# Interleaving the identity matmuls with the half-width matmuls of the SSD output, and moving two regions of on-chip memory

## The chip, the cores and the metric

The kernel runs on one core of a Trainium2 chip. The metric is the device time of one execution in microseconds (us), the median of three runs. Engines are named as in the profile: PE is TensorE's matmul side and PEld its loading of stationary operands, DVE is VectorE, ACT is ScalarE, POOL is GpSimd, SP issues the DMAs. A matmul here multiplies a stationary operand, which is loaded first, by a moving operand, which is streamed, and adds the product into a bank of PSUM, the accumulation memory. A 4-byte float matmul that is not marked as the reduced form appears as two passes in the trace.

## The reference

The program is one sequence of 256 tokens, width 1024, through two models' blocks: two layers with a three-branch attention mixer and two layers whose mixer joins multi-head latent attention with an SSD (state space) branch; every layer has a gated feed-forward before and behind the mixer. The change is in the SSD branch, whose scan works in two chunks of 128 tokens, four groups of eight heads:

```python
def step(state, inp):
    xc, dtc, bc, cc = inp
    acum = jnp.cumsum(dtc * a_g, axis=1)
    decay = jnp.exp(jnp.where(causal, acum[:, :, None] - acum[:, None, :], -jnp.inf))
    cb = jnp.einsum('btgn,bsgn->btsg', cc, bc)
    xdt = xc * dtc[..., None]
    y_diag = jnp.einsum('btsg,btsgh,bsghp->btghp', cb, decay, xdt)
    y_off = jnp.einsum('btgn,bghpn->btghp', cc, state) * jnp.exp(acum)[..., None]
    ...
    return new_state, y_diag + y_off
```

For the first chunk the state is zero and y_off vanishes; for the second chunk y is the sum of both terms.

## The kernel before

Twelve phases run one after the other: feed-forward (`ffn`), mixer (`m1` or `m2`), feed-forward, for each of four layers. The two `m2` phases hold the SSD branch. All weights, 459 MB, are streamed once through a ring of five buffers, RAW. Each weight is split into a high part WHI (ACT, line 1438) and a rest WLO (DVE, line 2342), and each product is three matmuls, high times high (L378), high times low (L379) and low times high (L380), with XH and XL the split activations; in `m2` phases a stretch of these weight matmuls stands between any two small steps. Each engine's instructions are written out by hand in their order; an engine waits on counters ("signals") that others raise. Nothing reorders them.

The SSD branch takes its four groups g one after the other. `sttr` (L1041) transposes the convolved input XSB through the identity matrix, which lies in CF; DVE makes XDT from it (L3072); `le` (L1066) spreads the cumulated decays, ACT exponentiates them, and DVE multiplies them with CBM into LE (L3088). `yp` (from L1068) then forms y for one group and one chunk c: for each of the four pairs of heads, b = 0 to 3, two matmuls (h = 0, 1) with a stationary operand of 64 columns of XDT, one writing PSUM partitions 0 to 63 and the other 64 to 127, each 128 columns wide (L1086). Pairs 0 and 1 lie in bank 2, pairs 2 and 3 in bank 3. The second chunk also needs y_off. DVE has left it in JUNK (L3081), tokens along the partitions, and four matmuls with JUNK as a full stationary operand of 128 columns and the identity as the moving one (L1080) turn it and put it into the same columns of the banks. So `yp` of the second chunk, in this text "the block", is 4 matmuls of the one kind and 8 of the other. There are 8 blocks: 4 groups in each of 2 phases.

Behind a block DVE reads the sum from the bank (`yw`, L3097, into WT), waiting for the block's last matmul; for group 3 ACT also waits for it (L2057). In the next group `yp` waits for LE (L3088) and `sttr` waits for XSB (L2931) or for XDT of the chunk before (L3072).

On-chip tensors are placed by hand by their byte address in a partition. Up from 16,512 follow RAW (WLO shares it), WHI, X, XH and XL; then JUNK; then the constants CF, CM and some small ones up to SM2; then, at M0, one overlay region of some 97 KB which each phase lays out for itself (SG, HF, HH, HL of the feed-forward; LE, XDT, XSB, YH, YL, OHA, OHB and others of the mixers).

Of the kernel before, what the change touches and what calls it, by code (L numbers as in the profile page):

```python
# [5 lines left out]
F32 = mybir.dt.float32  # L6
# [8 lines left out]
P = 128  # L15
# [75 lines left out]
class Signals:  # L91
# [10 lines left out]
    def up(self, name, *key, by=1):  # L102
        if name not in self.sem:
            self.sem[name], self.owner[name] = self.ctx.enter_context(self.nc.semaphore(name)), self.engine
            self.count[name] = 0
        assert self.owner[name] == self.engine, name
        self.count[name] += by
        if not self.known:
            assert not key or (name,) + key not in self.value, (name, key)
            self.value[(name,) + key] = self.count[name]  # L110
        return self.sem[name], by

    def at(self, name, *key):
        return (self.sem[name], self.value[(name,) + key]) if self.known else (None, 1)
# [21 lines left out]
class Counts:  # L136
# [6 lines left out]
    def before(self, member, distance):  # L143
# [33 lines left out]
M2_SQUARE = Counts([("lat", j, t) for j in range(3) for t in range(2)] + [("q", j, t) for j in range(3) for t in range(2)]  # L177
                   + [("k", t, h) for t in range(2) for h in range(2)] + [(kind, g) for g in range(4) for kind in ("wx", "yo")])
# [4 lines left out]
def build(nc, phases, x_in, pos_in, w_in, cf_in, cm1_in, cm2_in, out, ctx):  # L183
    START = 16512
    top = [START]

    def sb(name, shape, dt, at=None):
        n = 2 if dt == BF16 else 4
        for s in shape[1:]:
            n *= s  # L190
        n = (n + 31) // 32 * 32
        if at is None:
            at = top[0]
            top[0] += n
        ends.append((at + n, name))
        return nc.alloc_sbuf_tensor_at(name, shape, dt, offset=at)
# [5 lines left out]
    X = sb("X", [P, 2, D], F32)  # L202
    XH = sb("XH", [P, 8, 256], F32R)
    XL = sb("XL", [P, 8, 256], F32R)
    JUNK = sb("JUNK", [P, 2, 512], F32)
    CF = sb("CF", [P, CF_W], F32)
    CM = sb("CM", [P, CM1_W], F32)
    IDB = sb("IDB", [P, P], BF16)
# [7 lines left out]
    SM = sb("SM", [P, 512], F32)  # L216
    SM2 = sb("SM2", [P, 456], F32)
    KRD, WST, EAC, CWH, SNH = [SM2[:, a:z] for a, z in ((0, 256), (256, 288), (288, 320), (320, 440), (440, 456))]
    IDN, TRI, ONE = CF[:, C_IDN:C_IDN + P], CF[:, C_TRI:C_TRI + P], CF[:, C_ONE:C_ONE + P]
    M0 = top[0] + (START - top[0]) % 1024  # L220
    K = 1024

    def at_kb(kb):
        return M0 + int(kb * K)

# [37 lines left out]
    XDT = sb("XDT", [P, 2, 512], F32, at_kb(50))  # L263
# [5 lines left out]
    LE = sb("LE", [P, 2, 1024], F32, at_kb(58))  # L269
# [16 lines left out]
    PS = [ctx.enter_context(nc.psum_tensor(f"bank{i}", [P, 512], F32)) for i in range(8)]  # L286
# [67 lines left out]
    def m1_bank(j):  # L354
        return PS[6 if j == 2 else 4 + M1_BANK.index[j] % 2]

    def m2_bank(*m):
        return PS[4 + M2_BANK.index[m] % 3]
# [8 lines left out]
    class Tensor:  # L367
# [676 lines left out]
        def sts(self, n, g):  # L1044
# [4 lines left out]
            self.tr_free(n, "s", g)  # L1049
            e.matmul(PS[7][:, :], BTN[:, g, :], JUNK[:, M2_SQUARE.index[("wx", g)] % 2, :], start=True, stop=True).then_inc(*up("sts", n, g))  # L1050

# [17 lines left out]
        def yp(self, n, g, c):  # L1069
            e = self.e  # L1070
            e.wait_ge(*at("led", n, g, c))
            e.wait_ge(*at("xdt", n, g, c))
            if c == 0 and g:
                e.wait_ge(*at("yz", n, 4 * g - 1))
            if c == 1:
                e.wait_ge(*at("yo", n, g))
                yo = JUNK[:, M2_SQUARE.index[("yo", g)] % 2, :]
                for b in range(4):
                    col = (b % 2) * 256 + P
                    e.matmul(PS[2 + b // 2][:, col:col + P], yo[:, b * P:b * P + P], IDN, start=b % 2 == 0, stop=False)  # L1080
            for b in range(4):
                ps = PS[2 + b // 2]
                col = (b % 2) * 256 + c * P
                for h in range(2):
                    hh = 2 * b + h
                    ins = e.matmul(ps[64 * h:64 * h + 64, col:col + P], XDT[:, c, hh * 64:hh * 64 + 64], LE[:, c, hh * P:hh * P + P], start=c == 0, stop=c == 0 or b % 2 == 1)  # L1086
            ins.then_inc(*up("yp", n, g, c))

        def rms(self, n):
# [331 lines left out]
    class Scalar:  # L1421
# [158 lines left out]
        def psq(self, n, j):  # L1580
            e, q = self.e, M1_SQUARE.index[j] % 2
            e.wait_ge(*at("at", n, j, 1, 1))
            if M1_SQUARE.before(j, 2) is not None:
                e.wait_ge(*at("pss", n, M1_SQUARE.before(j, 2)))
            e.activation(JUNK[:, q, :], m1_bank(j)[:, :], ACT.Square).then_inc(*up("psq", n, j))

# [11 lines left out]
        def tev2(self, n):  # L1598
# [4 lines left out]
            e.wait_ge(*at("at", n, 2, 1, 1))  # L1603
            e.activation(JUNK[:, q, 0:128].rearrange("p (t d) -> p t d", t=2), src[:, :, 64:128], ACT.Square).then_inc(*up("psq", n, 2))
            e.copy(VT[:, :, 0:64], src[:, :, 128:192])
# [71 lines left out]
        def snsq(self, n, t):  # L1677
            e, q = self.e, M1_SQUARE.index[f"sn{t}"] % 2
            e.wait_ge(*at("ov", n, 11 if t else 7))
            e.wait_ge(*at("pss", n, M1_SQUARE.before(f"sn{t}", 2)))  # L1680
            e.activation(JUNK[:, q, :], OC[:, t, :], ACT.Square).then_inc(*up("psq", n, f"sn{t}"))

# [199 lines left out]
        def lsq(self, n, j):  # L1882
# [4 lines left out]
            for t in range(2):  # L1887
                i = M2_SQUARE.index[("lat", j, t)]
                e.activation(JUNK[:, i % 2, 0:256], m2_bank("bt", j)[:, t * 256:t * 256 + 256], ACT.Square, accum_out=SSC[:, 3 * t + j:3 * t + j + 1])
            e.copy(CQ[:, :, j * 256:j * 256 + 256], m2_bank("bt", j)[:, :]).then_inc(*up("tev", n, j))  # L1890
# [1978 lines left out]
```

## Time and profile before

| | us |
|---|---|
| median of 3 runs | 2800.02 (2795.24 to 2800.2) |
| the profiled execution's own time | 2800.02 |
| its span, first to last instruction | 2798.2 |
| PE busy | 2742.5 (98%) |
| DVE busy | 1791.2 (64%) |
| ACT busy | 1433.3 (51%) |
| POOL busy | 286.7 (10%) |
| mean granted TensorE clock, share of full | 0.993 |

The profiled execution is the median run itself; 1.8 us of its time lie outside its span. Busy time is a mean over phases with different limits, so the stretch around the change is read by itself below. Matmul ends are modelled and a matmul overlaps the next, so what one costs is read from the distance of two starts and not from its busy time.

### The profile page before, as it was taken

The numbers are of one execution on the slowest core, as the hardware profiler recorded it, in microseconds if no ns is written. First come the engines' busy times: TensorE is split into PE (matmuls) and PEld (weight loads), VectorE is DVE, ScalarE is ACT, GpSimd is POOL, SyncE is SP. The second block draws the span as 40 slices with busy tenths as digits, with TensorE's granted clock in tenths as the row PEclk, the third lists the DMA queues.
The fourth block names the chain that finished last, engine by engine and source line by source line (L and its number), as shares of the span: only waits on it lengthen the run. The fifth ranks groups of instructions, "written<-read, shape, count | busy, mean of one in ns | idle before, by whom it ended". The sixth has DMA issues, their size and how long they took to land.

```text
span 2798.2 us, 48877 instructions
## 1 busy us (share of the span) xinstructions
PE 2742.5 (98%) x20056; PEld 2569.8 (92%) x20056; DVE 1791.2 (64%) x3060; ACT 1433.3 (51%) x2441; POOL 286.7 (10%) x442
## 2 busy tenths in 40 slices
PE   8998999999998999999999999999999999999999
PEld 8998999999998999999998799999999988999998
DVE  5657857556467857556568788565565687875654
ACT  5445645444455644445446575354454465754543
POOL 0003301000003311000001212100000022111000
PEclk9999999999999999999999999999999999999999
DMA  5552344554542354545444234544454442345443
GB/s 206 185 202 108 121 174 165 191 200 171 191 177 106 124 180 182 188 174 196 181 158 165 78 135 157 187 181 185 168 194 181 170 168 80 133 165 181 166 183 149
DMA packets 64732, 462.02 MB, mean 165 GB/s; under 512 B 7296, under 2 KB 7808, under 8 KB 9344
## 3 DMA queue, kind: packets, MB, share of 16 engines
q1 hardware_dynamic: 64512, 458.90, 44.6%
q8 instruction: 160, 2.62, 0.4%
q14 instruction: 60, 0.49, 0.0%
HBM read 457.83 MB, written 1.05 MB: 164 GB/s over the span
## 4 chain that ended last, share of the span: by engine, by line
PE 82%; DVE 11%; ACT 2%; POOL 2%; issue 1%; DMA 1%; SPq 0%; DVEq 0%; POOLq 0%; ACTq 0%
PE bank L456 17%; PE bank L378 16%; PE bank L380 16%; PE bank L379 16%; PE bank L389 3%; PE bank L391 3%; PE bank L390 3%; PE bank L644 2%; DVE WLO L2342 2%; DVE CV L2919 2%; DMA RAW<-weights_dram 1%; POOL MTA L3501 1%; PE bank L422 1%; PE bank L556 1%; PE bank L1008 1%
## 5 line engine op out<-in xcount | busy, mean ns | idle before, releaser
L2342 DVE TENSOR_TENSOR WLO<-RAW,WHI 128x1024 fp32r<-128x1024 f32 (+1 forms) x872 | 1059.2, 1254 | 293.1 <-ACT WHI L1438 292.4
L1438 ACT CAST WHI<-RAW 128x1024 fp32r<-128x1024 f32 (+1 forms) x872 | 885.3, 1046 | 363.9 <-DMA RAW<-weights_dram 226.1
L378 PE MATMUL bank<-XH,WHI 128*128 128x256 f32 x3712 | 1060.2, 286 | 3.7 <-DVE WLO L2342 3.7
L379 PE MATMUL bank<-XL,WHI 128*128 128x256 f32 x3712 | 1051.5, 283 | 0.0
L380 PE MATMUL bank<-XH,WLO 128*128 128x256 f32 x3712 | 1051.5, 283 | 0.0
L378 PEld LDWEIGHTS bank<-XH,WHI 128*128 128x128 f32 x3712 | 712.8, 192 | 10.9 <-issue 3.0
L379 PEld LDWEIGHTS bank<-XL,WHI 128*128 128x128 f32 x3712 | 713.2, 192 | 5.1
L380 PEld LDWEIGHTS bank<-XH,WLO 128*128 128x128 f32 x3712 | 712.7, 192 | 0.0
L1502 ACT ACTIVATE SG<-bank 128x256 f32<-128x256 f32 x152 | 58.4, 384 | 487.1 <-PE bank L380 487.1
L2455 DVE TENSOR_TENSOR HF<-SG,bank 128x256 f32<-128x256 f32 x152 | 63.9, 421 | 339.1 <-ACT SG L1502 339.1
L389 PE MATMUL bank<-WHI,XH 128*128 128x256 f32 (+2 forms) x928 | 268.4, 289 | 5.8 <-DVE XL L2396 4.9
L391 PE MATMUL bank<-WHI,XL 128*128 128x256 f32 (+2 forms) x928 | 262.7, 283 | 0.0
L390 PE MATMUL bank<-WLO,XH 128*128 128x256 f32 (+2 forms) x928 | 262.7, 283 | 0.0
L456 PE MATMUL bank<-WHI,HH 128*128 128x512 f32 x704 | 219.4, 393 | 0.0
L456 PE MATMUL bank<-WLO,HH 128*128 128x512 f32 x704 | 217.8, 390 | 0.0
L456 PE MATMUL bank<-WHI,HL 128*128 128x512 f32 x704 | 217.4, 390 | 0.0
L389 PEld LDWEIGHTS bank<-WHI,XH 128*128 128x128 f32 x928 | 178.5, 192 | 8.4 <-issue 6.8
L390 PEld LDWEIGHTS bank<-WLO,XH 128*128 128x128 f32 x928 | 178.8, 193 | 0.4
L391 PEld LDWEIGHTS bank<-WHI,XL 128*128 128x128 f32 x928 | 178.5, 192 | 0.0
L456 PEld LDWEIGHTS bank<-WLO,HH 128*128 128x128 f32 x704 | 132.2, 188 | 29.0
L456 PEld LDWEIGHTS bank<-WHI,HL 128*128 128x128 f32 x704 | 132.2, 188 | 28.5
L456 PEld LDWEIGHTS bank<-WHI,HH 128*128 128x128 f32 x704 | 123.0, 189 | 17.0
(341 smaller groups left out, 3189.9 us busy)
## 6 DMA issues: line engine op xcount, KB each, us to landing
RAW<-weights_dram SPq DMA_DIRECT2D x431, 1024.0 KB, 4.8
RAW<-weights_dram SPq DMA_DIRECT2D x2, 800.0 KB, 4.2
X<-x_dram SPq DMA_DIRECT2D x2, 512.0 KB, 6.0
RAW<-weights_dram SPq DMA_DIRECT2D x2, 512.0 KB, 7.4
out_dram<-X SPq DMA_DIRECT2D x2, 512.0 KB, 2.7
RAW<-weights_dram SPq DMA_DIRECT2D x2, 384.0 KB, 3.2
CM<-mixer_dram SPq DMA_DIRECT2D x2, 320.5 KB, 9.8
CM<-mixer_dram SPq DMA_DIRECT2D x2, 176.0 KB, 5.3
```

What stands on the lines that cost most here:

```text
L378: self.e.matmul(bank, h, xh[:, x0 + k, :], start=k == k0, stop=False)
L379: self.e.matmul(bank, h, xl[:, x0 + k, :], start=False, stop=False)
L380: ins = self.e.matmul(bank, l, xh[:, x0 + k, :], start=False, stop=k == k1)
L389: self.e.matmul(bank, xh[:, x0 + k, xs], h, start=k == k0, stop=False)
L390: self.e.matmul(bank, xh[:, x0 + k, xs], l, start=False, stop=False)
L391: ins = self.e.matmul(bank, xl[:, x0 + k, xs], h, start=False, stop=k == k1)
L456: ins = e.matmul(PS[2 * t + nh][:, :], a[:, i % HR, t * P:t * P + P], w[:, c % s, col + nh * 512:col + nh * 512 + 512], start=i == 0 and w ...
L644: ins = e.matmul(PS[2 * t + h][:, :], a[:, k, xs], w[:, c % s, i * 1024 + h * 512:i * 1024 + h * 512 + 512], start=k == 0 and w is WHI and ...
L1438: e.copy(WHI[:, c % NHI, a:b], RAW[:, c % NLO, a:b]).then_inc(*up("hi", c, p))
L1502: e.activation(SG[:, i % 2, :], PS[5 - i % 2][:, 0:256], ACT.Silu).then_inc(*up("sg", n, i))
L2342: e.tensor_tensor(WLO[:, c % NLO, a:b], RAW[:, c % NLO, a:b], WHI[:, c % NHI, a:b].bitcast(F32), ALU.subtract).then_inc(*up("lo", c, p))
L2455: e.tensor_tensor(HF[:, r, :], SG[:, r, :], PS[5 - i % 2][:, 256:512], ALU.mult).then_inc(*up("hf", n, i))
```

## The change

Two things are changed.

The order inside the block. Before, the four identity matmuls stood first and the eight half-width ones behind them. Now each pair of heads has its identity matmul and then its own two half-width matmuls. The number of matmuls and their operands stay as they were; the start and stop flags, which say when an accumulation in PSUM begins and ends, are set per pair.

The placement. JUNK is allocated behind SM2 and not before CF, so its address rises from 114,816 to 125,920. CF to SM2 move down by 4,096 bytes. M0 was rounded up to lie at the same place in a 1,024-byte unit as 16,512, at 130,176, and is now the first free byte, 130,016: the whole overlay region moves down by 160 bytes. RAW, WLO, WHI, X, XH and XL stay.

```diff
@@ build
-    JUNK = sb("JUNK", [P, 2, 512], F32)
     CF = sb("CF", [P, CF_W], F32)
...
     SM2 = sb("SM2", [P, 456], F32)
...
+    JUNK = sb("JUNK", [P, 2, 512], F32)
...
-    M0 = top[0] + (START - top[0]) % 1024
+    M0 = top[0]
@@ Tensor.yp
             if c == 1:
                 e.wait_ge(*at("yo", n, g))
-                yo = JUNK[:, M2_SQUARE.index[("yo", g)] % 2, :]
-                for b in range(4):
-                    col = (b % 2) * 256 + P
-                    e.matmul(PS[2 + b // 2][:, col:col + P], yo[:, b * P:b * P + P], IDN, start=b % 2 == 0, stop=False)
             for b in range(4):
                 ps = PS[2 + b // 2]
                 col = (b % 2) * 256 + c * P
+                if c == 1:
+                    e.matmul(ps[:, col:col + P], JUNK[:, M2_SQUARE.index[("yo", g)] % 2, b * P:b * P + P], IDN, start=True, stop=False)
                 for h in range(2):
                     hh = 2 * b + h
-                    ins = e.matmul(ps[64 * h:64 * h + 64, col:col + P], XDT[...], LE[...], start=c == 0, stop=c == 0 or b % 2 == 1)
+                    ins = e.matmul(ps[64 * h:64 * h + 64, col:col + P], XDT[...], LE[...], start=c == 0, stop=True)
```

In the changed file the identity matmul is L1081 and the half-width ones are L1084. On TensorE, the first block of the first `m2` phase stands in a row before as follows (destination, then moving and stationary operand):

```order
L380 MATMUL bank5<-XH_53,WLO_50 128x256
L1080 MATMUL bank2<-CF_56,JUNK_55 128x128 x2
L1080 MATMUL bank3<-CF_56,JUNK_55 128x128 x2
L1086 MATMUL bank2<-LE_108,XDT_102 64x128 x4
L1086 MATMUL bank3<-LE_108,XDT_102 64x128 x4
L1041 MATMUL bank7<-CF_56,XSB_120 128x128 x4
```

And the same place now:

```order
L380 MATMUL bank5<-XH_53,WLO_50 128x256
L1081 MATMUL bank2<-CF_55,JUNK_67 128x128
L1084 MATMUL bank2<-LE_108,XDT_102 64x128 x2
L1081 MATMUL bank2<-CF_55,JUNK_67 128x128
L1084 MATMUL bank2<-LE_108,XDT_102 64x128 x2
L1081 MATMUL bank3<-CF_55,JUNK_67 128x128
L1084 MATMUL bank3<-LE_108,XDT_102 64x128 x2
L1081 MATMUL bank3<-CF_55,JUNK_67 128x128
L1084 MATMUL bank3<-LE_108,XDT_102 64x128 x2
L1041 MATMUL bank7<-CF_55,XSB_120 128x128 x4
```

The order within a kind is kept; what was one run of each kind is now four runs of each. The last block of the second `m2` phase is followed by weight matmuls on TensorE. Before:

```order
L380 MATMUL bank4<-XH_53,WLO_50 128x256
L1080 MATMUL bank2<-CF_56,JUNK_55 128x128 x2
L1080 MATMUL bank3<-CF_56,JUNK_55 128x128 x2
L1086 MATMUL bank2<-LE_108,XDT_102 64x128 x4
L1086 MATMUL bank3<-LE_108,XDT_102 64x128 x4
L378 MATMUL bank5<-XH_53,WHI_51 128x256
```

Now:

```order
L380 MATMUL bank4<-XH_53,WLO_50 128x256
L1081 MATMUL bank2<-CF_55,JUNK_67 128x128
L1084 MATMUL bank2<-LE_108,XDT_102 64x128 x2
L1081 MATMUL bank2<-CF_55,JUNK_67 128x128
L1084 MATMUL bank2<-LE_108,XDT_102 64x128 x2
L1081 MATMUL bank3<-CF_55,JUNK_67 128x128
L1084 MATMUL bank3<-LE_108,XDT_102 64x128 x2
L1081 MATMUL bank3<-CF_55,JUNK_67 128x128
L1084 MATMUL bank3<-LE_108,XDT_102 64x128 x2
L378 MATMUL bank5<-XH_53,WHI_51 128x256
```

What stands ahead of and behind the block has not moved. The other engines' instructions keep their order, and `yp` of the first chunk is unchanged.

## Rows read from the trace of the kernel before

**Rows 1.** Page: busy time by engine, then the chain that ended last by engine.
```profile
PE 2742.5 (98%) x20056; PEld 2569.8 (92%) x20056; DVE 1791.2 (64%) x3060; ACT 1433.3 (51%) x2441; POOL 286.7 (10%) x442
...
PE 82%; DVE 11%; ACT 2%; POOL 2%; issue 1%; DMA 1%; SPq 0%; DVEq 0%; POOLq 0%; ACTq 0%
```

**Rows 2.** Windows: stretch, length, busy PE, PEld, DVE, ACT, POOL, clock, DMA share, GB/s.
```profile
1678.00:1709.00 31.00, 29.99 (x261) 27.97 (x260) 27.43 (x44) 22.66 (x47) 5.86 (x5) 1.00 0.37 137
1709.00:1730.00 21.00, 21.00 (x183) 20.66 (x182) 17.44 (x32) 10.89 (x16) 4.08 (x5) 1.00 0.45 156
```

**Rows 3.** Line 1080: count, duration ns least/median/most, first and last start.
```profile
L1080 PE MATMUL bank<-CF,JUNK x64: 272/275/331, 1626.7 to 2471.3; 128*128 128x128 f32 x64
```

**Rows 4.** Timeline of PE, first block: start, length, instructions merged with count.
```profile
1626.58 0.28 PE L380 MATMUL bank<-XH,WLO 128*128 128x256 f32 x1
1626.70 1.06 PE L1080 MATMUL bank<-CF,JUNK 128*128 128x128 f32 x8
1627.69 1.09 PE L1086 MATMUL bank<-LE,XDT 128*64 128x128 f32 x16
1628.71 0.65 PE L1041 MATMUL bank<-CF,XSB 128*128 128x128 f32 x4
```

**Rows 5.** Timeline of PEld, the loads of the same block.
```profile
1626.58 0.98 PEld L1080 LDWEIGHTS bank<-CF,JUNK 128*128 128x128 f32 x8
1627.68 0.85 PEld L1086 LDWEIGHTS bank<-LE,XDT 128*64 128x64 f32 x16
```

**Rows 6.** Timeline of PE, attention scores that change between 128 and 64 rows.
```profile
1581.00 0.65 PE L1007 MATMUL bank<-KN,QN 128*128 128x256 f32 x2
1581.58 0.70 PE L1008 MATMUL bank<-KP,QP 64*128 64x256 f32 x2
1582.21 0.23 PE L1009 MATMUL bank<-CMB,IDB 128*128 128x128 bf16 x1
```

**Rows 7.** Timelines of DVE, PE and ACT: who reads a block's sum, and when.
```profile
1629.14 0.48 DVE L3097 SCALAR_TENSOR_TENSOR WT<-XSB,CM,bank 128x256 f32<-128x256 f32 x1
...
1647.98 1.09 PE L1086 MATMUL bank<-LE,XDT 128*64 128x128 f32 x16
...
1650.85 0.47 DVE L3097 SCALAR_TENSOR_TENSOR WT<-XSB,CM,bank 128x256 f32<-128x256 f32 x1
...
1711.04 0.60 ACT L2057 ACTIVATE GT<-bank 128x512 f32<-128x512 f32 x1 [0.94 <-PE bank L1086]
```

**Rows 8.** Waits of PE, 1620 to 1712: us in total, times, longest.
```profile
PE bank L1041 <- DVE XDT L3072: 1.2, 2, 1.0
PE bank L1086 <- DVE LE L3088: 0.4, 1, 0.4
PE bank L1041 <- DVE XSB L2931: 0.2, 1, 0.2
```

**Rows 9.** Timeline of PE at its longest waits, idle time in brackets.
```profile
1694.55 0.28 PE L380 MATMUL bank<-XH,WLO 128*128 128x256 f32 x1
1695.84 0.63 PE L1041 MATMUL bank<-CF,XSB 128*128 128x128 f32 x4 [1.01 <-DVE XDT L3072]
...
2403.01 0.66 PE L1086 MATMUL bank<-LE,XDT 128*64 128x128 f32 x8 [0.66 <-DVE LE L3088]
```

**Rows 10.** Timeline of PE, moving operands 200 and 96 columns wide.
```profile
213.44 0.28 PE L389 MATMUL bank<-WHI,XH 128*128 128x200 f32 x1
...
214.78 0.27 PE L389 MATMUL bank<-WHI,XH 128*128 128x200 f32 x1
...
1473.66 0.28 PE L389 MATMUL bank<-WHI,XH 128*128 128x96 f32 x1
...
1475.00 0.28 PE L389 MATMUL bank<-WHI,XH 128*128 128x96 f32 x1
```

**Rows 11.** Groups by form, DVE: line, tiles, count | busy us, mean ns.
```profile
L2919 DVE SCALAR_TENSOR_TENSOR CV<-bank,SM,CV 128x255 f32<-128x255 f32 x48 | 20.9, 477 | 11.5 <-ACT CV L1918 11.3
...
L2898 DVE SCALAR_TENSOR_TENSOR CQL<-bank,CM,CQH 128x256 fp32r<-128x256 f32 x12 | 5.2, 477 | 0.1
```

More of the change, by code:

```diff
@@ L1083, in yp @@
                 col = (b % 2) * 256 + c * P
+                if c == 1:
+                    e.matmul(ps[:, col:col + P], JUNK[:, M2_SQUARE.index[("yo", g)] % 2, b * P:b * P + P], IDN, start=True, stop=False)
                 for h in range(2):
                     hh = 2 * b + h
-                    ins = e.matmul(ps[64 * h:64 * h + 64, col:col + P], XDT[:, c, hh * 64:hh * 64 + 64], LE[:, c, hh * P:hh * P + P], start=c == 0, stop=c == 0 or b % 2 == 1)
+                    ins = e.matmul(ps[64 * h:64 * h + 64, col:col + P], XDT[:, c, hh * 64:hh * 64 + 64], LE[:, c, hh * P:hh * P + P], start=c == 0, stop=True)
             ins.then_inc(*up("yp", n, g, c))
```

## The prediction

> **What bounds the kernel now.** I read the page first: PE is busy 98% of the span and makes up 82% of the chain that ended last, DVE 11% [rows 1]. So a microsecond added to TensorE's order is a microsecond of the kernel, unless TensorE would have waited anyway behind it. Busy time cannot tell that, so I then read the stretch of the SSD groups by windows. Between two blocks, 1678 to 1709 us, PE is busy 29.99 of 31.00 us and DVE 27.43 of 31.00: both are close to the limit, and about 1 us of slack lies there. From 1709 us on, PE is busy 21.00 of 21.00 us: no slack [rows 2]. The waits of PE in the whole stretch of the first `m2` phase are few: 1.2 us in two waits for XDT, 0.4 for LE, 0.2 for XSB [rows 8]. Last come the starts in the timeline around a block, which give the price of each matmul.
>
> **The change part by part: the order.** The trace has 64 passes of line 1080, which is 8 blocks of 4 matmuls in 2 passes [rows 3]; each block has 16 half-width passes beside them [rows 4]. None is added or removed. What changes is how often TensorE goes over from a full 128-column stationary operand to a pair of 64-column ones and back. Before, a block went over once and back once. Now it goes over four times and back four times: 3 more of each, 6 more changes.
>
> The price of one change comes from the first block [rows 4]. The eight full passes have a merged length of 1.06 us. One alone lasts 0.275 [rows 3], so seven steps take 0.785, 0.112 each. From the first of them to the first half-width pass it is 0.99 us, so the step across the change is 0.99 - 0.785 = 0.205, or 0.09 more than a step inside the run. The half-width passes run two at a time: eight pairs have a length of 1.09, less one pass of 0.275 that is 0.815 for seven steps, 0.116 each and 0.04 us over seven steps of 0.11. The step back is 1.02 - 0.815 = 0.205, again 0.09 too long, and the four passes behind it have a length of 0.65, so their three steps take 0.375, 0.045 more than three of 0.11. A change costs 0.09 + 0.04 = 0.13 on the way over and 0.09 + 0.045 = 0.135 on the way back.
>
> The trace has runs as short as the new ones elsewhere: in the attention scores, runs of two 256-column passes alternate between 128 and 64 rows. They start 0.58 and 0.63 us apart [rows 6], where two passes of twice the width of 0.11 us would need 0.44. So a short run pays 0.14 to 0.19 us per change. I take 0.15, which lies between this and the block's own 0.13: 6 x 0.15 = 0.9 us per block. As bounds I keep nothing (if the next operand's load could hide the change) and 6 x 0.19 = 1.15.
>
> Whether a load can hide it shows beside the passes. Ahead of the block the load of JUNK starts at 1626.58, together with the matmul before and 0.12 us ahead of its own at 1626.70. The load of XDT starts at 1627.68, with its own matmul at 1627.69 and 0.2 us behind the last full pass [rows 4, 5]. Nothing was loaded ahead across the change. Two rules of the Trainium skill pull apart here. "TensorE: Matmul & The Clock Gate" (section on the array's architecture, engine queue depths) lets TensorE pull a weight load ahead of matmuls in flight; by that alone the new order would cost nothing and the time would stay 2800.0. "TensorEngine Tiling (Array Packing)" (Key Properties) says that changing the tiling mode drains the engine, which would be paid six more times in every block. The trace agrees with the second at this place, with the 0.2 us step, and with the first only inside a run.
>
> **How much of 0.9 us per block reaches the end.** After each block I look for what TensorE waits for next, and whether that was itself held up by the block.
>
> Block 1 (1626.70). Its sum is complete at 1627.69 + 1.09 = 1628.78 [rows 4]; DVE reads it at 1629.14 [rows 7], 0.36 us later. With 0.9 more, DVE starts 0.54 late. DVE then works almost without a gap up to LE, for which PE waits 0.4 us by the waits [rows 8]. PE alone would carry 0.9 - 0.4 = 0.5, DVE carries 0.54. The shift is 0.54.
>
> Block 2 (ends at 1647.98 + 1.09 = 1649.07; DVE reads it at 1650.85, 1.78 us later [rows 7]). DVE is not touched. PE then waits for XSB, 0.2, and for XDT, 1.2 - 1.0 = 0.2 [rows 8]. The idle time in brackets is short of what a start shows: before the long wait the step is 1695.84 - 1694.55 = 1.29 against 0.12 between weight matmuls, so 1.17 lost where the view has 1.01 [rows 9]. With 0.16 added to each wait, 0.2 + 0.2 + 0.32 = 0.7 is absorbed (0.65 before rounding). The shift is 0.25.
>
> Block 3. PE waits 1.17 us for XDT at 1695.84 [rows 9], behind a DVE queue that takes the block's sum as late as in block 2. All of the 0.9 is absorbed: 0.
>
> Block 4. ACT waits for this block (0.94 us at 1711.04 [rows 7]), and PE has no idle time behind it [rows 2]. The shift is 0.9.
>
> Sum for the phase: 0.54 + 0.25 + 0 + 0.9 = 1.7 us. The second `m2` phase has the same instructions; its wait for LE is 0.66 instead of 0.4 [rows 9], which does not help, as DVE's 0.54 decides. So 2 x 1.7 = 3.4 us.
>
> **The flags.** A start on the second matmul of a bank and a stop on each pair change what is kept in the accumulator's state, not the number of columns that are streamed. The weight matmuls start a new sum once in 24 matmuls and their step is 0.12 us at either. Nothing.
>
> **The placement.** The large streams do not move: RAW, WLO, WHI, XH, XL keep their addresses, and so do the rows that make up most of the time. The 4,096-byte move keeps every alignment up to that size. The overlay's 160 bytes and JUNK's 11,104 put tensors that lay on a multiple of 64 bytes at 32 bytes off it. The trace has this state already: a moving operand of WHI 200 columns wide is 800 bytes, so every second slice begins 32 bytes off a multiple of 64. Twelve such passes take 214.78 - 213.44 = 1.34 us, and twelve 96 columns wide, which all begin on a multiple of 64, take 1475.00 - 1473.66 = 1.34 us [rows 10]. On DVE, line 2919 writes and reads CV from 4 bytes off with 477 ns a piece, and the aligned line 2898 takes 477 ns for one column more [rows 11]. I take nothing. The bound: the two stretches agree within 0.01 us, which is 0.0017 for each of six unaligned passes, and some 3,800 passes have an operand in the overlay (2,112 of the down projection, the rest in the output projections). That is 6.5 us at most, up or down; no row shows a stationary operand or an ACT read at such an address.
>
> **Sum.** Profiled span 2798.2 + 3.4 = 2801.6, and 1.8 us lie outside the span: 2803.4 us. The profiled execution took 2800.02, which is the median of the three runs, so the sum stands against either.
>
> **Rivals.**
> The switch is free (0.12). TensorE would load the next operand while the last run drains. For it: loads run ahead inside a run. Against: the load at 1627.68 did not [rows 5]. Time 2800.0.
>
> Nothing is absorbed, slower (0.20). DVE is 27.43 of 31.00 busy [rows 2], and if its queue depends on the block's sum more than I read, or on the weight matmuls behind it which come 0.9 us late, then the waits of PE move along with PE. This decides from 1.8 us of delay per block at DVE's read of the sum, the margin of block 2 [rows 7], or where ACT, which feeds DVE, had been waiting for PE. Then 8 x 0.9 = 7.2 us and 2807.2; at the upper price of 1.15 it is 9.2 and 2809.2.
>
> The placement costs (0.09). Unaligned stationary operands of the down projection load more slowly than their matmul streams. At the bound 6.5 us on top: 2809.9, or 2806 to 2807 at half of it.
>
> The placement gains (0.07). Two tensors that TensorE reads at once no longer lie at the same place in a 1,024-byte unit. For it there is no row, against it the equal steps of rows 10. At the bound, 2803.4 - 6.5 = 2796.9, and below 2794.4 only if it is more than that.
>
> **How the numbers follow.** My forecast holds 0.52, and its own range is 2801.5 to 2805, from a change at 0.13 to 0.19 us with the same absorption. About 0.2%, or 5.6 us, is what a measurement of this kernel can tell from no change; the three runs before lie 5 us apart. The forecast and the free switch are within it, apart from a small part of the forecast that measurement lifts over it. Of the other cases nothing absorbed and the costly placement are mostly over it. Within: 0.50 + 0.12 + 0.03 = 0.65. Slower: 0.02 + 0.20 + 0.07 = 0.29. Faster: 0.06. The range reaches from the gain by placement at its bound to nothing absorbed at 0.15 to 0.19 us a change: 2797 to 2808.5.
>
> **What would show each step.** In the changed profile a block should be four runs of two full passes and four of four half-width ones, some 2.9 us from its first start to what follows, where it was 2.01 to the transposes [rows 4]. The wait at 1695.84 should be there with about 0.1 us instead of 1.01. The read of block 1's sum by DVE should have a wait for PE of about 0.5 us, where none is now. Steps between the down projection's matmuls and DVE's mean times should be the same. I am wrong if a block's length stays at 2.0 us, if the phase's shift is 3.6 us rather than 1.7, or if the feed-forward phases, which hold nothing of the new order, differ by more than 1 us.

## The result, and the profile after

The forecast of no measurable change was wrong: the changed kernel takes 2816.7 us (median of 4 runs, 2814.66 to 2819.82) against 2799.18 (2795.24 to 2800.2) for the kernel before. The ratio is 1.0066, with a 95% interval of 1.0049 to 1.0084; that is 17.5 us more, where 3.4 were forecast. The time lies outside the range of 2797 to 2808.5. The profiled execution took 2815.74 us, its span is 2813.8, and the mean granted clock is 0.993 of full speed, as before.

The page of the kernel after, busy time by engine and the chain that ended last, to be read beside [rows 1]:

```profile
PE 2762.2 (98%) x20056; PEld 2572.7 (91%) x20056; DVE 1791.9 (64%) x3060; ACT 1433.7 (51%) x2441; POOL 283.7 (10%) x442
...
PE 86%; DVE 8%; ACT 2%; POOL 2%; issue 1%; DMA 1%; SPq 0%; DVEq 0%; POOLq 0%; ACTq 0%
```

PE has the same 20,056 instructions and is busy 19.7 us longer. The others hardly changed: PEld gained 2.9 us, DVE 0.7 and ACT 0.4. So the time came on TensorE, in the same instructions, and not as a wait.

The first block of the first `m2` phase on PE in the kernel after (start, length, merged count), to be read beside [rows 4]:

```profile
1630.96 0.28 PE L380 MATMUL bank<-XH,WLO 128*128 128x256 f32 x1
1631.08 0.39 PE L1081 MATMUL bank<-CF,JUNK 128*128 128x128 f32 x2
1631.40 0.44 PE L1084 MATMUL bank<-LE,XDT 128*64 128x128 f32 x4
1631.77 0.49 PE L1081 MATMUL bank<-CF,JUNK 128*128 128x128 f32 x2
...
1634.13 0.65 PE L1041 MATMUL bank<-CF,XSB 128*128 128x128 f32 x4
```

From the block's first start to the transposes it is 1634.13 - 1631.08 = 3.05 us; before it was 2.01. That is 1.04 more for six changes of width, 0.173 each. The loads of the same block after, to be read beside [rows 5]:

```profile
1631.40 0.20 PEld L1084 LDWEIGHTS bank<-LE,XDT 128*64 128x64 f32 x4
1631.77 0.30 PEld L1081 LDWEIGHTS bank<-CF,JUNK 128*128 128x128 f32 x2 [0.17 <-issue]
1632.18 0.20 PEld L1084 LDWEIGHTS bank<-LE,XDT 128*64 128x64 f32 x4
```

At every change the load starts with its own matmul (1631.40, 1631.77), in both directions, and PEld stands idle 0.17 us ahead of the load of JUNK. In all 8 blocks, every load that follows a change starts at most 3 ns ahead of its own matmul; a JUNK load that follows a 128-column weight matmul starts 0.12 us ahead. Nothing is loaded ahead across a change.

Behind the blocks, the kernel after on DVE, PE and ACT (the row of PE's start is the long wait of [rows 9], that of ACT the last of [rows 7]):

```profile
1634.25 0.48 DVE L3095 SCALAR_TENSOR_TENSOR WT<-XSB,CM,bank 128x256 f32<-128x256 f32 x1 [0.64 <-PE bank L1084]
...
1700.90 0.28 PE L380 MATMUL bank<-XH,WLO 128*128 128x256 f32 x1
1701.25 0.63 PE L1041 MATMUL bank<-CF,XSB 128*128 128x128 f32 x4
...
1717.47 0.60 ACT L2055 ACTIVATE GT<-bank 128x512 f32<-128x512 f32 x1 [1.98 <-PE bank L1084]
```

DVE now waits 0.64 us for block 1's sum, where it had none. PE's wait of 1.01 us for XDT is gone: the step is 1701.25 - 1700.90 = 0.35, where it was 1.29. ACT waits 1.98 us for block 4, 1.04 more than before, which is the whole lengthening of the block. This part went about as forecast, so the missing 14 us had to be elsewhere. The windows of the same work after (columns as in [rows 2]) say the same:

```profile
1683.50:1714.50 31.00, 30.93 (x260) 28.19 (x259) 27.53 (x44) 22.74 (x48) 5.85 (x5) 1.00 0.37 137
1714.50:1735.50 21.00, 21.00 (x174) 19.84 (x173) 16.48 (x29) 10.01 (x16) 3.88 (x4) 1.00 0.41 151
```

PE has 0.07 us idle in the first stretch, where it had 1.01. No PE wait is left there to absorb more.

What had changed outside the blocks shows in the groups by form. Before, for the down projection (line, tiles, count | busy us, mean ns of one):

```profile
L456 PE MATMUL bank<-WHI,HH 128*128 128x512 f32 x704 | 219.4, 393 | 0.0
L456 PE MATMUL bank<-WLO,HH 128*128 128x512 f32 x704 | 217.8, 390 | 0.0
L456 PE MATMUL bank<-WHI,HL 128*128 128x512 f32 x704 | 217.4, 390 | 0.0
...
L644 PE MATMUL bank<-WLO,MH 128*128 128x512 f32 x64 | 19.8, 390 | 0.0
L644 PE MATMUL bank<-WLO,XH 128*128 128x512 f32 x64 | 19.8, 390 | 0.0
```

After, the same five groups (L644 is an output projection of the mixers):

```profile
L456 PE MATMUL bank<-WHI,HH 128*128 128x512 f32 x704 | 222.0, 396 | 0.0
L456 PE MATMUL bank<-WLO,HH 128*128 128x512 f32 x704 | 222.0, 397 | 0.0
L456 PE MATMUL bank<-WHI,HL 128*128 128x512 f32 x704 | 221.2, 395 | 0.0
...
L644 PE MATMUL bank<-WLO,MH 128*128 128x512 f32 x64 | 20.1, 396 | 0.0
...
L644 PE MATMUL bank<-WLO,XH 128*128 128x512 f32 x64 | 19.8, 390 | 0.0
```

The first three hold 2,112 passes; their busy time rose from 654.6 to 665.2 us, 10.6 us, though their operands' shapes, their count and their order are unchanged. All three have their stationary operand (HH, HL) in the overlay, and their moving operand of 512 columns in WHI or WLO. In L644, with the same moving operand WLO, the passes whose stationary operand moved (MH) went from 390 to 396 ns, and those whose stationary operand did not (XH) stayed at 390. YH, YL, OHA, OHB, OLA and OLB lie in the overlay too, but they are the moving operands of output projections of 256 columns (L378 to L380). Those steps did not change in the mean (0.1203 us before, 0.1204 after).

The length of a phase shows it more simply. Every phase begins with transposes at line 422. Counted from 0, phases 8 and 9 are feed-forwards. Their first starts, before:

```profile
1839.90 0.27 PE L422 MATMUL bank<-CF,XS 128*128 128x128 f32 x1
...
2029.22 0.27 PE L422 MATMUL bank<-CF,XS 128*128 128x128 f32 x1
```

And after:

```profile
1846.86 0.27 PE L422 MATMUL bank<-CF,XS 128*128 128x128 f32 x1
...
2037.40 0.27 PE L422 MATMUL bank<-CF,XS 128*128 128x128 f32 x1
```

That is 189.32 us before and 190.54 after, for a feed-forward phase that holds no instruction of the new order. There are eight such phases, so some 9.7 us. (Read one by one, seven are 1.2 to 1.3 us longer. The first is not, 194.03 us after 194.35, but PE's longest wait at the start of the program was 4.9 us in the profile before and 3.4 in this one.) Below, "the phase" is phase 8. In the profiles of before, `order_only`, `junk_only` and `identity_half`, which leave the overlay where it was, it takes 189.29 to 189.32 us, while mixer phase 10 takes 382.6 to 387.4; that makes it a much finer scale than the total.

### The profile page after: what moved, and what is told of

Its sections match the earlier page's. It is cut to its first block, busy times and chain, and to the rows that moved or that the text cites. A ratio compares the mean times of both kernels' runs of the same rounds, so it can differ in the third digit from the quotient of the medians.

```text
span 2813.8 us, 48877 instructions
## 1 busy us (share of the span) xinstructions
PE 2762.2 (98%) x20056; PEld 2572.7 (91%) x20056; DVE 1791.9 (64%) x3060; ACT 1433.7 (51%) x2441; POOL 283.7 (10%) x442
## 4 chain that ended last, share of the span: by engine, by line
PE 86%; DVE 8%; ACT 2%; POOL 2%; issue 1%; DMA 1%; SPq 0%; DVEq 0%; POOLq 0%; ACTq 0%
PE bank L456 17%; PE bank L378 17%; PE bank L380 17%; PE bank L379 17%; PE bank L389 3%; PE bank L391 3%; PE bank L390 3%; PE bank L644 2%; DVE WLO L2340 2%; POOL MTA L3499 1%; PE bank L1084 1%; PE bank L422 1%; DMA RAW<-weights_dram 1%; ACT PBA L1650 1%; PE bank L1008 1%
## 5 line engine op out<-in xcount | busy, mean ns | idle before, releaser
L378 PE MATMUL bank<-XH,WHI 128*128 128x256 f32 x3712 | 1060.7, 286 | 3.7 <-DVE WLO L2340 3.7
L380 PE MATMUL bank<-XH,WLO 128*128 128x256 f32 x3712 | 1051.4, 283 | 0.0
L378 PEld LDWEIGHTS bank<-XH,WHI 128*128 128x128 f32 x3712 | 712.5, 192 | 11.2 <-issue 3.1
L380 PEld LDWEIGHTS bank<-XH,WLO 128*128 128x128 f32 x3712 | 712.7, 192 | 0.0
L456 PE MATMUL bank<-WHI,HH 128*128 128x512 f32 x704 | 222.0, 396 | 0.0
L456 PE MATMUL bank<-WLO,HH 128*128 128x512 f32 x704 | 222.0, 397 | 0.0
L456 PE MATMUL bank<-WHI,HL 128*128 128x512 f32 x704 | 221.2, 395 | 0.0
L456 PEld LDWEIGHTS bank<-WHI,HL 128*128 128x128 f32 x704 | 133.4, 189 | 32.0
L456 PEld LDWEIGHTS bank<-WLO,HH 128*128 128x128 f32 x704 | 132.3, 188 | 32.0
L456 PEld LDWEIGHTS bank<-WHI,HH 128*128 128x128 f32 x704 | 122.7, 189 | 19.5
```

The costliest lines, as they stand in the source:

```text
L378: self.e.matmul(bank, h, xh[:, x0 + k, :], start=k == k0, stop=False)
L380: ins = self.e.matmul(bank, l, xh[:, x0 + k, :], start=False, stop=k == k1)
L456: ins = e.matmul(PS[2 * t + nh][:, :], a[:, i % HR, t * P:t * P + P], w[:, c % s, col + nh * 512:col + nh * 512 + 512], start=i == 0 and w ...
```

## The experiments

All are compared with the kernel before on the same chip. Theory P (placement): the overlay's new address costs most of it. Theory O (order): the changes of width cost more than the blocks show.

### The parts alone: order, M0, JUNK

`order_only`, the new order with the old addresses:

```diff
-    M0 = top[0]                       # and JUNK back in front of CF
+    M0 = top[0] + (START - top[0]) % 1024
```

> Only the order inside the block is changed; JUNK and the overlay region lie where they lay before. Theory (the cost has two parts: the changes of operand width, and the overlay region's address): each of the 8 blocks is about 1.03 us longer, of which some is absorbed, so 4 to 5 us more than before (ratio 1.0014 to 1.0018), and the down projection's step stays at 0.227 us. Rival (the order alone makes the kernel 0.6% slower, the placement nothing): 15 to 17 us more.

Measured: 2803.38 us against 2798.91, ratio 1.0016 [1.0007, 1.0025], the phase 189.29. The ends of a block and of DVE's wait in `order_only`:

```profile
1623.84 0.28 PE L380 MATMUL bank<-XH,WLO 128*128 128x256 f32 x1
...
1627.01 0.66 PE L1041 MATMUL bank<-CF,XSB 128*128 128x128 f32 x4
...
1627.13 0.48 DVE L3095 SCALAR_TENSOR_TENSOR WT<-XSB,CM,bank 128x256 f32<-128x256 f32 x1 [0.65 <-PE bank L1084]
```

From the matmul ahead of the block to the transposes it is 3.17 us, against 2.13 before. The order alone costs 4.5 us (2.0 to 7.0), and the forecast's 3.4 lies in that.

The stretch from the first block of an `m2` phase to the next feed-forward is a finer scale for this part, as the phase is for the placement. Its ends in the kernel before are 1626.70 [rows 4] and 1839.90 us, so 213.20 us. In `order_only`:

```profile
1623.96 0.39 PE L1081 MATMUL bank<-CF,JUNK 128*128 128x128 f32 x2
...
1839.26 0.27 PE L422 MATMUL bank<-CF,XS 128*128 128x128 f32 x1
```

That is 215.30 us, 2.10 more. By the starts of the blocks, block 1 passes on 0.74 us, block 2 0.32, block 3 nothing and block 4 1.04. The second `m2` phase went from 213.52 to 215.29 us, 1.77 more; in `junk_only`, which has the old order, it takes 213.20. So the order costs 3.9 us, or 4.2 against `junk_only`.

`m0_only`, the old order with the overlay 160 bytes lower:

```diff
-    M0 = top[0] + (START - top[0]) % 1024
+    M0 = top[0]
```

> The order and JUNK as before; only the overlay region starts at 130,016 and not at 130,176. Theory (stationary operands at 32 bytes off a multiple of 64 cost TensorE time): the down projection's step rises from 0.227 to about 0.234 us, 2,112 passes, so 10 to 12 us more than before (ratio 1.004). Rival (it was JUNK's new place, or the order): no change, step 0.227.

Measured: 2811.01 us, ratio 1.0045 [1.0032, 1.0057], that is 12.1 us (9.0 to 16.0). The down projection in `m0_only` begins so:

```profile
1908.83 0.63 PE L456 MATMUL bank<-WHI,HH 128*128 128x512 f32 x2
1909.30 0.63 PE L456 MATMUL bank<-WLO,HH 128*128 128x512 f32 x2
1909.77 0.39 PE L456 MATMUL bank<-WHI,HL 128*128 128x512 f32 x1
```

And in the kernel before:

```profile
1902.07 0.63 PE L456 MATMUL bank<-WHI,HH 128*128 128x512 f32 x2
1902.54 0.62 PE L456 MATMUL bank<-WLO,HH 128*128 128x512 f32 x2
1903.00 0.39 PE L456 MATMUL bank<-WHI,HL 128*128 128x512 f32 x1
```

Four steps take 0.94 us instead of 0.93. The mean step from one pass of the down projection to the next is 0.2340 instead of 0.2287 us: too little to see in one pass, 11 us over all 2,112. A little of it is gained back beside them: in phase 3, 1.36 us more in these steps and 0.13 less in the gate matmuls make the phase 1.22 longer. The phase is 190.53, and its L456 groups read as those of the kernel after.

`junk_only`, with JUNK moved behind SM2 and M0 still at 130,176:

```diff
-    JUNK = sb("JUNK", [P, 2, 512], F32)
     CF = sb("CF", [P, CF_W], F32)
...
     SM2 = sb("SM2", [P, 456], F32)
+    JUNK = sb("JUNK", [P, 2, 512], F32)
```

> The order as before and the overlay region at 130,176 as before; JUNK lies behind SM2 and CF to SM2 lie 4,096 bytes lower. Theory: no change within 0.1%, since JUNK is read by TensorE in a few matmuls only and the others keep their alignment. Rival (CF's or JUNK's address is what costs): 10 us more.

Measured: 2798.53 us, ratio 0.9999 [0.999, 1.0008], the phase 189.31: nothing. The three parts add up to 4.5 + 12.1 - 0.4 = 16.2 us, of the 17.5 measured together. Theory P holds for the larger part, theory O only at the size of the forecast.

### The price of a change of width

`identity_half` has the new order and the old addresses, but splits each identity matmul into two of 64 columns, so that the whole block stays at half width:

```diff
-    e.matmul(ps[:, col:col + P], JUNK[..., b * P:b * P + P], IDN, start=True, stop=False)
+    for h in range(2):
+        e.matmul(ps[64 * h:64 * h + 64, col:col + P], JUNK[..., b * P + 64 * h:b * P + 64 * h + 64], IDN, start=True, stop=False)
```

> Placement as before, order interleaved as in the changed kernel, but each identity matmul is split into two of 64 stationary columns, one for each half of the partitions, so the block stays at one width throughout. Theory (what costs 0.15 to 0.17 us is the change between 128 and 64 columns, not that different matmuls alternate, nor the flags): a block is about as long as before, 2.0 to 2.2 us and not 3.1, and the time is that of before within 0.1%. Rival (alternating sources or setting start per pair costs): 3.0 us a block and 4 to 5 us more in all.

Measured: 2799.97 us against 2798.5, ratio 1.0002 [0.9993, 1.0011]. A block in `identity_half`:

```profile
1626.19 0.28 PE L380 MATMUL bank<-XH,WLO 128*128 128x256 f32 x1
1626.40 0.44 PE L1082 MATMUL bank<-CF,JUNK 128*64 128x128 f32 x4
1626.67 0.39 PE L1085 MATMUL bank<-LE,XDT 128*64 128x128 f32 x4
...
1628.30 0.66 PE L1041 MATMUL bank<-CF,XSB 128*128 128x128 f32 x4
```

It has the same alternation of operands, banks and flags, and takes 2.11 us, as the block before (2.13) and not 3.17. Within its blocks each run's load starts 0.107 us ahead of its matmul, where `order_only` has at most 0.003. So it is the change of width that costs, not the alternation. "TensorEngine Tiling (Array Packing)" of the Trainium skill (Key Properties) says that changing the tiling mode drains the engine; this pair of kernels agrees, at 0.173 us a change.

### Which tensors make the placement cost

`hh_back` is the whole change with only HH, HL and XS put back to their old addresses:

```diff
-    HH = sb("HH", [P, HR, 256], F32R, at_kb(4))
+    HH = sb("HH", [P, HR, 256], F32R, at_kb(4) + 160)     # HL at_kb(10), XS at_kb(16) likewise
```

> The whole change, but with HH, HL and XS 160 bytes further up within the overlay region, where they lay before; the rest of the overlay keeps its new place. Theory (the cost of the placement is in HH and HL as stationary operands of the down projection): the down projection's step is 0.227 to 0.229 us again, a feed-forward phase takes 189.3 us and not 190.5, and what is left is the order's 4 to 5 us (ratio 1.0015 to 1.002). In the same run MH and ML stay at the new place and keep their slow step of 0.234. Rival (another tensor of the overlay, or the feed-forward's ACT and DVE writes, carries it): 190.5 us a phase, ratio near 1.006.

Measured: 2806.2 us, ratio 1.0023 [1.0015, 1.0032]; the phase is 189.38 and blocks are 3.17. Its groups by form:

```profile
L456 PE MATMUL bank<-WHI,HH 128*128 128x512 f32 x704 | 219.4, 393 | 0.0
L456 PE MATMUL bank<-WHI,HL 128*128 128x512 f32 x704 | 217.4, 390 | 0.0
L644 PE MATMUL bank<-WLO,MH 128*128 128x512 f32 x64 | 20.1, 396 | 0.0
```

HH and HL are as before; MH, left at its new address, is still slow. Of 17.5 us some 10 are undone by three tensors, two of which are the down projection's stationary operands. What is left is 7.7 us (4 to 9): the order's 4.5, and some 3 that may be the output projections and what else moved. Of these 3, the trace shows 1.2 us in the steps of the 192 passes on MH and ML; the rest isn't attributed and lies within the noise.

### What about the address it is

`m0_aligned_64` puts M0 at 130,048, a multiple of 64; `m0_130208`, `m0_130304`, `m0_130240` and `m0_130432` put it 32, 128, 64 and 256 bytes above the old place. Each has the old order.

```diff
-    M0 = top[0] + (START - top[0]) % 1024
+    M0 = top[0] + 32         # m0_aligned_64; 192, 288, 224 and 416 in the other four
```

> The order and JUNK as before; the overlay region starts at 130,048, a multiple of 64 and of 128, but not at the same place in a 1,024-byte unit as the weights. Theory (alignment to 64 is what counts): as before, step 0.227 us. Rival (what counts is that stationary and moving operands lie at the same place in a 1,024-byte unit): slower by about 11 us as with 130,016, step 0.234 us.

Measured: 2806.13 us against 2798.91, ratio 1.0028 [1.0017, 1.0038], the phase 190.07. A multiple of 64 still costs 7.2 us, and 130,048 is even a multiple of 1,024. So that the overlay lay 32 bytes off a multiple of 64, which the prediction had looked at, is not the cause.

> Order and JUNK as before, the overlay region at 130,208, which is 32 bytes above before: 32 off a multiple of 64, and only 32 bytes from the old relation to the weights. If 32 bytes off 64 costs by itself: a feed-forward phase about 0.5 us longer than 189.29 (the difference between 130,016 and 130,048), or the full 1.2. If only the distance between stationary and moving operand within 1,024 bytes counts, and smoothly: 0 to 0.3 us.

Measured: 2806.17 us against 2798.5, ratio 1.0024 [1.0015, 1.0033], the phase 190.23.

> Order and JUNK as before, the overlay region at 130,304, which is 128 bytes above before and a multiple of 64 and 128. Before was 0, 130,048 (128 bytes below) cost 0.75 us in a feed-forward phase. If distance from the weights' place in a 1,024-byte unit counts symmetrically: 0.7 to 0.8 us a phase, time +5 to +7 us. If alignment alone counted: 0. If the sign of the distance counts: some other value, perhaps less than before.

Measured: 2804.11 us, ratio 1.0015 [1.0006, 1.0025], the phase 190.07: the same phase as 128 bytes below.

> Order and JUNK as before, overlay at 130,240, 64 bytes above before. If a multiple of 64 is aligned enough and the distance counts smoothly: 0.3 to 0.5 us a phase more than before, less than the 0.91 of 32 bytes above. If any distance from the old place costs as much: 0.75 us, as at 128 bytes on either side.

Measured in one execution with a profile: 2808.78 us. First starts of phases 8 and 9 in `m0_130240`:

```profile
1842.26 0.27 PE L422 MATMUL bank<-CF,XS 128*128 128x128 f32 x1
...
2032.62 0.27 PE L422 MATMUL bank<-CF,XS 128*128 128x128 f32 x1
```

The phase is 190.36.

> Order and JUNK as before, overlay at 130,432, 256 bytes above before. 128 above and 128 below cost the same (0.75 us a phase). If what counts repeats every 256 bytes: 189.29 us a phase, as before. If it is a distance within 1,024 bytes whose best points are 0 and 512: 0.8 us longer or more.

Measured in one execution with a profile: 2802.9 us, which as a single total tells little. The phase does, in `m0_130432`:

```profile
1838.87 0.27 PE L422 MATMUL bank<-CF,XS 128*128 128x128 f32 x1
...
2028.19 0.27 PE L422 MATMUL bank<-CF,XS 128*128 128x128 f32 x1
```

It is 189.32, exactly that of before: a shift of 256 bytes costs nothing.

### A step of 512 bytes: a theory that fell

In the kernel before, the steps of the down projection's passes on the first half of the 256 tokens are slightly longer in the mean (0.2304 us; 0.2309 if each step is counted to the pass that follows it, as the expectations below do) than those on the second half (0.2267), and the halves of HH lie 512 bytes apart. If that were the address, putting all pieces at one place would make all steps the longer or all the shorter one. `split_512` gives each half 1,024 bytes of its own and uses its upper 512; `split_0` uses the lower 512. Both have the old order and M0.

```diff
-    HH = sb("HH", [P, HR, 256], F32R, at_kb(4))
+    HH = sb("HH", [P, HR, 2, 256], F32R, at_kb(24))       # HL likewise, at_kb(4), XS at_kb(36); split_0: 0:128 below
...
-    ins = e.matmul(PS[2 * t + nh][:, :], a[:, i % HR, t * P:t * P + P], ...)
+    ins = e.matmul(PS[2 * t + nh][:, :], a[:, i % HR, t, 128:256], ...)
```

> Order, JUNK and overlay start as before. HH and HL get a row pitch of 1,024 bytes for each half of 128 tokens, with every piece at 512 bytes within it, so that each stationary operand of the down projection lies 512 bytes (modulo 1,024) from the moving operand that streams while it is loaded. In before, these pairs step at 0.2267 us and the pairs at distance 0 at 0.2309. Theory (the distance within 1,024 bytes sets the step): all at 0.2267, a feed-forward phase 0.4 to 0.5 us shorter than 189.29, 3.5 to 4 us less in all (ratio 0.9985 to 0.9988), faster than before. Rival (the 0.2309 belongs to the first token half itself, not to its address): 189.3 us a phase, no change.

> The same as split_512 with every piece at 0 bytes in its 1,024, so that every distance is 0. Theory: all steps 0.231 us, a feed-forward phase about 0.5 us longer than 189.29, time about 4 us more than before. Rival (token half, not address): 189.3 us.

Measured: 2798.26 and 2799.48 us against 2799.04, ratios 0.9997 [0.9988, 1.0006] and 0.9999 [0.999, 1.0009]; the phase is 189.32 and 189.31. The theory fell: 0 and 512 bytes are the same, and the difference between the halves goes with the half, not with its address: it is 0.2304 against 0.2267 us in both kernels.

### Own address, or distance between the two operands

So far the overlay moved and the weights stood still. In all of these kernels, two things change together: the stationary operand's own place, and its distance from the weights. `all_up_128` moves the weights and the overlay up by 128 bytes; `weights_up_128` moves the weights and leaves the overlay at 130,176. In both, X, XH, XL, JUNK and the constants move with the weights.

```diff
-    START = 16512
+    START = 16640
     ...
-    M0 = top[0] + (START - top[0]) % 1024
+    M0 = top[0] + 32         # weights_up_128 only
```

> Order as before. Everything, weights and overlay, lies 128 bytes higher: weights from 16,640, overlay at 130,304, so their distance is 0 modulo 256 as before, while the overlay's own address is the one that cost 0.75 us a phase when it moved alone. If the distance between stationary and moving operand counts: 189.29 us a phase, time as before. If the overlay's own address modulo 256 counts: 190.0 to 190.1 us a phase, 5 to 7 us more.

> Order as before. The weights, X, XH and XL lie 128 bytes higher, the overlay stays at 130,176, its address of before. If the distance counts: 190.0 to 190.1 us a phase, 5 to 7 us more. If the overlay's own address counts: 189.29 us a phase, as before.

Measured: `all_up_128` 2798.42 us against 2800.99, ratio 0.9994 [0.9985, 1.0003]; `weights_up_128` 2804.84, ratio 1.0014 [1.0005, 1.0024]. First starts of phases 8 and 9 in `all_up_128`:

```profile
1839.84 0.27 PE L422 MATMUL bank<-CF,XS 128*128 128x128 f32 x1
...
2029.15 0.27 PE L422 MATMUL bank<-CF,XS 128*128 128x128 f32 x1
```

And in `weights_up_128`:

```profile
1842.39 0.27 PE L422 MATMUL bank<-CF,XS 128*128 128x128 f32 x1
...
2032.46 0.27 PE L422 MATMUL bank<-CF,XS 128*128 128x128 f32 x1
```

189.31 against 190.07. Every operand of `all_up_128` has a new address and nothing is slower; in `weights_up_128` HH and HL have their old address and the passes are slower. It is the distance that counts. `m0_aligned_64` completes the square: with the weights and the overlay each at 0 or at 128 modulo 256, the phase is short where the two agree (before, `all_up_128`) and long where they differ (`m0_aligned_64`, `weights_up_128`). Line 644 of `weights_up_128` holds the comparison within one kernel:

```profile
L644 PE MATMUL bank<-WLO,MH 128*128 128x512 f32 x64 | 20.1, 394 | 0.0
...
L644 PE MATMUL bank<-WLO,XH 128*128 128x512 f32 x64 | 19.8, 390 | 0.0
```

XH moved with the weights and is as before; MH stayed where it was and is slower. All points together:

| weights to overlay, modulo 256 bytes | kernels | the phase, us | more than before | mean step between two down-projection passes, us | mean step of the 256-column passes on overlay operands, us |
|---|---|---|---|---|---|
| 0 | before, all_up_128, m0_130432 | 189.32, 189.31, 189.32 | 0 | 0.2287 | 0.1203 |
| 32 | m0_130208 | 190.23 | 0.91 | 0.2328 | 0.1181 |
| 64 | m0_130240 | 190.36 | 1.04 | 0.2335 | 0.1182 |
| 96 (160 below) | after, m0_only | 190.54, 190.53 | 1.21 | 0.2340 | 0.1204 |
| 128 | m0_aligned_64, m0_130304, weights_up_128 | 190.07, 190.07, 190.07 | 0.75 | 0.2318 | 0.1192 |

Three kernels at 128 come to it from below, from above and by moving the other operand, and agree within 0.01 us. The rows at 32, 64 and 96 rest on one direction of the overlay each.

The last column goes the other way. It holds the 1,536 output-projection passes whose moving operand lies in the overlay and whose stationary operand is a weight. Their step is shortest at 32 and 64, and at 0 and 96 it is the same within 0.1 ns. One of their groups before:

```profile
L379 PE MATMUL bank<-YL,WHI 128*128 128x256 f32 x256 | 72.4, 283 | 0.0
```

And in `m0_130208`:

```profile
L379 PE MATMUL bank<-YL,WHI 128*128 128x256 f32 x256 | 71.2, 278 | 0.0
```

So no distance is the best for all work: 0 is the best measured for the down projection, and 32 bytes for these, by 3.5 us in all. These passes differ from the down projection's in their width and in which operand moved, and no experiment separates the two.

## Why the prediction was wrong, point by point

**The step that failed is the placement:** "I take nothing", with a bound of 6.5 us. It measured 12.1 us, two thirds of the whole. It failed in two ways.

The rows chosen could not show it. [Rows 10] compare two stretches of passes whose *moving* operand is 200 or 96 columns wide. In both, the step is 0.11 us and does not depend on the width, so something other than the width of the moving operand sets it. The step at stake was that of a pass of 512 columns, 0.23 us, beside the load of a stationary operand that had moved against it. The prediction said that "no row shows a stationary operand" at such an address, and nonetheless took nothing and drew the bound from the rows that it had; such a bound does not hold for work of another kind.

The question was the wrong one. The prediction asked whether each tensor is still aligned by itself. `m0_aligned_64` and `all_up_128` show that this isn't what counts. The line that was removed rounded M0 to the same place as START, modulo 1,024: the diff itself named a relation between two tensors. One rival did look at it ("two tensors that TensorE reads at once no longer lie at the same place"), and gave it 0.07 as a *gain*. The relation was right and its sign was wrong: for the down projection the same place is the fast one. At other distances such a gain exists in part (3.5 us in the output projections of `m0_130208`), but not at the 96 of this change. The rival that the placement costs had the place right (the down projection's stationary operands) and a price at half of what came.

**The order's part was right.** A change of width was taken at 0.15 us, between 0.13 and 0.19, and measured 0.173; a block grew by 1.04 us instead of 0.9. `order_only` took 2803.38 us, where the forecast of this part was 2803.4; its share, 4.5 us (2.0 to 7.0), agrees with 3.4 but can't confirm it to the microsecond. By the stretches of the trace it is 3.9 to 4.2 us. That the price comes from the change of width is shown by `identity_half`.

**The absorption was right.** DVE's new wait at block 1 was forecast at about 0.5 us and is 0.64, as the block grew by 0.14 more. Of the 1.04 us of each of the four blocks, 0.30, 0.72, 1.04 and 0 are absorbed; of the forecast's 0.9 it was to be 0.36, 0.65, 0.9 and 0. That 2.10 us are passed on, and not 1.7, comes from the larger growth of the block. Block 3's wait for XDT took its share: the step fell from 1.29 to 0.35. Block 4 passed everything on to ACT: 0.94 became 1.98. For the second phase the prediction said that the longer wait for LE, 0.66 us, would not help; against the profile before, it did, as 1.77 us came through there and not 2.10.

**The other rivals.** "The switch is free" fell: the blocks and PEld's starts refute it, and `identity_half` shows the free form. "Nothing is absorbed" fell as well: its 8 x 1.04 = 8.3 us lie above `order_only`'s interval and are twice what the trace shows, and the wait at block 3 is gone. For JUNK and the 4,096 bytes of the constants, "nothing" was right.

**The signs named beforehand** worked. The prediction said that it is wrong if the feed-forward phases differ by more than 1 us: they differ by 1.2.

**What stays open.** Why the distance counts inside the chip wasn't settled. A stationary operand is being loaded while the previous pass streams its moving operand, so both are read from on-chip memory at once; that the two disturb each other at unlike places in a 256-byte unit is argued, not shown. Distances of 160 to 224 bytes weren't measured. Of the 12.1 us, the eight feed-forward phases account for 9.7. In the profiles of before and `m0_only` the four mixers are 2.8 us longer together, but single mixer phases differ by more than that between kernels of the same placement; only the 1.2 us of MH and ML were identified there.

## What to carry to other kernels

Treat the addresses of two tensors that TensorE reads at once as one quantity: before a region is repacked to save bytes, ask which stationary operands it holds, which wide moving operands they meet, and whether the rounding that is removed tied the two together. Don't take the same place for a rule, though: here it was the best for one kind of pass and not for another. Keep matmuls of one stationary width together, or split the wide ones to the narrow width; each change costs 0.17 us where TensorE has no idle time behind it. A bound must come from rows of the same kind as the work that it bounds; where there are none, the range has to be wider than the nearest other kind suggests.

## What the runs showed of the hardware

- The step of a 512-column pass with a 128-column stationary operand depends on the distance between the two operands' addresses modulo 256 bytes: 0.2287 us at 0, up to 0.2340 at 96, the largest measured. "SBUF — State Buffer" of the Trainium skill (Who interferes with whom) gives TensorE two independent read ports, one for the moving operand and one for the weight load, and says that it never waits on anyone. By that the overlay's address would cost nothing; the measurement differs by 12.1 us in 2,800. The section is about different engines that get in each other's way, and no run here tells whether it is the port or something behind it.
- The step of a 256-column pass whose moving operand lies in the overlay depends on the distance too, and otherwise: 0.1203 us at 0, 0.1181 at 32, 0.1182 at 64, 0.1204 at 96 and 0.1192 at 128.
- Going over between a stationary operand of 128 columns and a pair of 64 costs 0.173 us in a run of short turns, and no load is started ahead of it: at most 3 ns, against 107 ns where the width stays the same.
- A feed-forward phase of 189 us repeats within 0.05 us between the profiles of kernels with the same placement, so that a difference of 0.4% of it is plain in one profile, while the totals of single executions of one kernel differ by 5 to 9 us.
